# Expert mixture in a bidirectional encoder: V row weights built per four rows, and three more row buffers

## The reference

```
q = (xb @ wq)                      # 8 heads, 2 halves of 128
s = q . keys                       # 128 scores per half
top 16 of each half, top 16 of the 256 sums -> idx: 128 experts per token
gate = softmax(best)
act  = gelu(einsum('ted,td->te', u_tab[idx], xb)) * gate
out  = einsum('te,ted->td', act, v_tab[idx])
y    = rmsnorm(h + out)
```

## Time and profile before

| | us |
|---|---|
| median of 3 runs | 3148.33 |
| lowest, highest | 3132.29, 3150.12 |
| profiled execution, span from first to last instruction | 3149.3 |
| PE busy (matmul) | 2885.8 (92%) |
| PEld busy | 1456.1 (46%) |
| DVE busy | 1640.8 (52%) |
| ACT busy | 571.5 (18%) |
| POOL busy | 1538.7 (49%) |
| bytes moved | 1006.58 MB, mean 320 GB/s |

### The profile page before, as it was taken

The page is one execution under the profiler, slowest core; times in us unless marked ns, Lnnn a source line. Parts: engine busy times, 40 slices in busy tenths (PEclk is TensorE's granted clock), DMA queues, the critical chain, the costliest instruction groups (busy, mean ns, idle before and its releaser), DMA issues.

```text
span 3149.3 us, 30263 instructions
## 1 busy us (share of the span) xinstructions
PE 2885.8 (92%) x10618; PEld 1456.1 (46%) x10618; DVE 1640.8 (52%) x3896; ACT 571.5 (18%) x1212; POOL 1538.7 (49%) x1334
## 2 busy tenths in 40 slices
PE   6999989678999979956799999999999999999997
PEld 4656647433334445534344444444444444444442
DVE  5331125774887746887355654444655544444442
ACT  4111122110104556656000000000000000000000
POOL 3111213364565535655556565555555555555544
PEclk9999999899999999977899999999999999999999
DMA  4332264497999989999999999999999999999987
GB/s 150 110 104 74 87 213 143 140 372 259 334 392 355 367 339 382 364 343 404 400 367 376 384 385 366 379 381 378 385 388 394 382 368 376 384 369 390 373 335 293
DMA packets 341662, 1006.58 MB, mean 320 GB/s; under 512 B 32295, under 2 KB 110887, under 8 KB 338952
## 3 DMA queue, kind: packets, MB, share of 16 engines
q0 software_dynamic: 184320, 671.17, 56.0%
q1 hardware_dynamic: 155464, 308.32, 27.9%
q10 hardware_dynamic: 1728, 25.17, 1.9%
HBM read 958.13 MB, written 46.40 MB: 319 GB/s over the span
## 4 chain that ended last, share of the span: by engine, by line
PE 63%; DMA 9%; DVE 3%; issue 2%; POOL 1%; another core or an unknown queue 1%; ACT 1%; SPq 1%; POOLq 0%; DVEq 0%; ACTq 0%
PE job_ps L1627 20%; PE wide_ps L1611 19%; PE v_ps L1653 8%; PE job_ps L678 4%; PE wide_ps L678 4%; DMA v_rows<-in_peer_v,row_t 3%; PE gate_ps L678 2%; DMA u_row<-in_peer_u,row_u 2%; DMA arena<-in_peer_v 1%; DVE u_row L1870 1%; DMA hand<-tmp_gates 1%; PE job_ps L1599 1%; PE wide_ps L1599 1%; POOL v_rows L1535 1%
## 5 line engine op out<-in xcount | busy, mean ns | idle before, releaser
L1535 POOL DMA_INDIRECT v_rows<-in_peer_v,row_t x622 | 679.3, 1092 | 849.7 <-PE v_ps L1653 692.6
L1870 DVE CUSTOM_DVE_ANT_0 u_row<-u_row,x_tile 128x1024 f32<-128x1024 f32 x640 | 774.5, 1219 | 316.5 <-DMA u_row<-in_peer_u,row_u 287.2
L1520 POOL DMA_INDIRECT u_row<-in_peer_u,row_u x640 | 723.9, 1131 | 256.9 <-issue 191.8
L1627 PE MATMUL job_ps<-arena 128*128 128x512 f32 x1536 | 692.5, 599 | 8.2 <-issue 4.1
L1611 PE MATMUL wide_ps<-hand,arena 128*128 128x384 f32 x2048 | 687.5, 489 | 0.0
L1611 PEld LDWEIGHTS wide_ps<-hand,arena 128*128 128x128 f32 x2048 | 384.3, 190 | 317.7 <-issue 79.1
L1627 PEld LDWEIGHTS job_ps<-arena 128*128 128x128 f32 x1536 | 287.9, 191 | 376.2 <-issue 339.5
L1653 PE MATMUL v_ps<-v_rows,diag 128*32 128x512 f32 x2488 | 347.4, 613 | 44.2 <-DMA v_rows<-in_peer_v,row_t 40.8
L1912 DVE TENSOR_TENSOR arena<-arena,job_ps 128x512 f32<-128x512 f32 x192 | 131.2, 684 | 408.6 <-PE job_ps L1627 336.8
L948 POOL TENSOR_TENSOR exact<-arena,exact 128x1024 fp32r<-128x1024 f32 x48 | 116.7, 2436 | 437.7 <-ACT exact L690 437.7
L1760 ACT ACTIVATE hand<-wide_ps 128x384 f32<-128x384 f32 x128 | 62.7, 490 | 1413.9 <-PE wide_ps L1611 1176.0
(11 more groups left out here) (292 smaller groups left out, 2487.2 us busy)
## 6 DMA issues: line engine op xcount, KB each, us to landing
arena<-in_peer_ut SPq DMA_DIRECT2D x128, 512.0 KB
arena<-in_peer_v SPq DMA_DIRECT2D x128, 512.0 KB
hand<-tmp_gates SPq DMA_DIRECT2D x32, 768.0 KB
tmp_gates<-arena ACTq DMA_DIRECT2D x10, 2048.0 KB
arena<-in_w_in SPq DMA_DIRECT2D x32, 512.0 KB, 3.6
hand<-in_w_in SPq DMA_DIRECT2D x32, 512.0 KB
x_tile<-tmp_xn SPq DMA_DIRECT2D x80, 128.0 KB
u_row<-in_peer_u,row_u POOLq DMA_INDIRECT x640
```

What stands on the lines that cost most here:

```text
L1520: pool.indirect_dma_start(u_row[n % NU][:], None, dram["peer_u"], bass.IndirectOffsetOnAxis(row_u[g % 2][:, e:e + 1], 0)).then_inc(u_in[n ...
L1535: pool.indirect_dma_start(v_row[b], None, dram["peer_v"], bass.IndirectOffsetOnAxis(row_t[g % 3][:, t:t + 1], 0)).then_inc(v_in[b], 16)
L1627: last = pe.matmul(job_ps[q % 2][:], actd[g % 2][:, jj, d * P:(d + 1) * P], vw[j % NO][:, half * 512:(half + 1) * 512], start=jj == 0, sto ...
L1870: dve.tensor_tensor_reduce(out=u_row[n % NU][:], in0=u_row[n % NU][:], in1=xb[h_ % 2][:], scale=1.0, scalar=0.0, op0=ALU.mult, op1=ALU.add ...
```

## The change

`diag` goes, with ACT's zeroing of it. `turn_act` is followed by `keep_act(h)`, a copy of the turned activations (128x32) into a ring of eight, `act_t`. For each quad DVE then does `pick(n)`: it multiplies a slice of `unit_col`, a row of zeros with a one at place 31, by the four activation columns of the quad (128x4, broadcast over 32), which gives the four 128x32 weights, in one of `NP` = 4 small tiles `picked`. The quad waits for its pick (`picked_done`, once a quad, where `diag_done` was waited for once in eight). Pick n waits for `keep_act` of its 32 rows and for the quad four before it (`v_used`). In DVE's order it stands at beat 41 + 4n, ahead of the adds, dense steps and dot of that beat. The memory goes to the row buffers: `NU` 6 to 7, `NV` 7 to 9, and 16 instead of 13 for the last V rows.

```diff
-    NU, NV, NSC, NW, NO = 6, 7, 2, 3, 6
+    NU, NV, NSC, NW, NO = 7, 9, 2, 3, 6
+    NP, NH = 4, 8
...
-        diag = m.sb("diag", [P, Q, 32 * 32])
+        act_t = m.sb("act_t", [P, NH * QT])
+        unit_col = m.sb("unit_col", [P, 63])
+        picked = [m.sb(f"picked{b}", [P, Q, 32]) for b in range(NP)]
...
             def quad(n):
                 g, k = n // 32, n % 32
-                c = k % 8 * 4 + k // 8
-                if k % 8 == 0:
-                    pe.wait_ge(diag_done, n // 8 + 1)
+                pe.wait_ge(picked_done, n + 1)
...
-                        last = pe.matmul(v_ps[half][32 * q:32 * q + 32, :], diag[:, q, 32 * c:32 * c + 32],
+                        last = pe.matmul(v_ps[half][32 * q:32 * q + 32, :], picked[n % NP][:, q],
                                          v_row[v_home(r)][:, half * 512:(half + 1) * 512], start=k == 0, stop=k == 31)
...
-            act.activation(diag[:].rearrange("p q (a b) -> p (q a) b", b=P),
-                           R.iota[:].unsqueeze(1).broadcast_to([P, 32, P]), ACT.Copy, scale=0.0).then_inc(cleared, 1)
...
-            def set_diag(h):
+            def keep_act(h):
                 dve.wait_ge(act_turned, h + 1)
-                if h >= 4:
-                    dve.wait_ge(v_used, (h - 3) * QT)
+                if h >= NH:
+                    dve.wait_ge(picked_done, (h - NH + 1) * 8)
+                dve.tensor_copy(act_t[:, h % NH * QT:(h % NH + 1) * QT], act_ps).then_inc(act_t_done, 1)
+
+            def pick(n):
+                h, at = n // 8, n % 8
+                c = at * 4 + h % 4
+                dve.wait_ge(act_t_done, h + 1)
+                if n >= NP:
+                    dve.wait_ge(v_used, Q * (n - NP + 1))
                 else:
-                    dve.wait_ge(cleared, 1)
-                dve.tensor_copy(diag[:, :, 33 * (h % 4)::132], act_ps.rearrange("p (q c) -> p q c", q=Q)).then_inc(diag_done, 1)
+                    dve.wait_ge(unit_set, 2)
+                mine = act_t[:, h % NH * QT:(h % NH + 1) * QT].rearrange("p (q c) -> p q c", q=Q)[:, :, at:at + 1]
+                dve.tensor_tensor(picked[n % NP][:], unit_col[:, 31 - c:63 - c].unsqueeze(1).broadcast_to([P, Q, 32]),
+                                  mine.broadcast_to([P, Q, 32]), ALU.mult).then_inc(picked_done, 1)
...
+            dve.memset(unit_col[:], 0.0).then_inc(unit_set, 1)
+            dve.wait_ge(unit_set, 1)
+            dve.memset(unit_col[:, 31:32], 1.0).then_inc(unit_set, 1)
...
                     if n == GEL_AT[h_] + 5:
-                        set_diag(h_)
+                        keep_act(h_)
+                if n >= LAG - 1 and (n - LAG) % Q == Q - 1 and (n + 1 - LAG) // Q < ROWS // Q:
+                    pick((n + 1 - LAG) // Q)
```

More of the change, by code:

```diff
@@ L1380, in second_and_experts @@
         rows_u_done, gates_turned, gate_q_done = (m.sem(f"e_{n}") for n in ("rows_u_done", "gates_turned", "gate_q_done"))
-        exp_done, gel_done, act_done, act_turned, diag_done, v_used, lead_done, gate_done = (m.sem(f"e_{n}") for n in (
-            "exp_done", "gel_done", "act_done", "act_turned", "diag_done", "v_used", "lead_done", "gate_done"))
+        exp_done, gel_done, act_done, act_turned, act_t_done, picked_done, v_used, lead_done, gate_done = (m.sem(f"e_{n}") for n in (
+            "exp_done", "gel_done", "act_done", "act_turned", "act_t_done", "picked_done", "v_used", "lead_done", "gate_done"))
         sel_turned, sel_copied, a_done, sq_done, b_done, d_done, hot_used, evicted = (m.sem(f"e_{n}") for n in (
@@ L1386, in second_and_experts @@
             "u_used", "gel_read", "weighted", "job_done", "summed"))
-        added, ms, root, inv, normed, stored, cleared, pre_gone = (m.sem(f"e_{n}") for n in (
-            "added", "ms", "root", "inv", "normed", "stored", "cleared", "pre_gone"))
+        added, ms, root, inv, normed, stored, unit_set, pre_gone = (m.sem(f"e_{n}") for n in (
+            "added", "ms", "root", "inv", "normed", "stored", "unit_set", "pre_gone"))
         order, unit, held = [], 0, ()
@@ L1634, in turn_act @@
                 turn_free()
-                tr_reader[:] = [diag_done, h + 1]
+                tr_reader[:] = [act_t_done, h + 1]
                 for j in range(4):
```

## The result

The changed kernel takes 3111.98 us (median of 5, 3104.07 to 3123.68) against 3145.37 us of before (median of 5). The ratio is 0.9906, 95% interval 0.9878 to 0.9935: about 0.9% faster. 3106 was forecast, within 3065 to 3147. The profiled execution spans 3113.9 us where the one before spanned 3149.3, 35.4 us less.

What follows compares the result with a forecast made beforehand. PE's matmuls were taken to bound the dense stretch, 96.6% of 1600 to 3000 us. The terms -14 (dense stretch), -20 (600 to 1600 us) and -8 (tail) sum to -42 us: 3106 us against a median of 3148.3, range 3065 to 3147.

Steps and rivals of the forecast that it cites:

- the dense stretch: 1600 to 3000 us: one quad more of lead removes most of 16.3 us of landing waits, -14 us (ends 0 and -48).
- the early part: 600 to 1600 us: POOL, its U gathers and DVE get further ahead; -13 and -10 with +3 for picks, -20 us.
- the tail: From 3000 us: 16 homes instead of 13 let the last V gathers issue without a stop, -8 us (ends 0 and -12).
- What bounds the kernel: 1600 to 3000 us: unchanged matmul time fills 1352 of 1400 us, so at most 48 us can go.
- the -10 given to the engines' unused share: 600 to 1300 us: a fifth of the 48 us that the transfer engines leave unused is gained, -10 us.
- the 13 us of the way to 404 GB/s: 1300 to 1600 us: half of the 19 us up to the best slice's rate, plus the three-row reserve, -13 us.
- The step on POOL: Tail: the last 37 V gathers at 1.26 us each, 45 us to the start of the last instead of 53.6.
- Picks: Weights on DVE: 160 picks of 0.28 us, 45 us, just in time where DVE is late; charged 3 us (ends 0 and 15).
- U buffer: U buffers 6 to 7: nothing of its own; keeps U from becoming the next stop as POOL runs ahead.
- transfers are the bound: Rival, chance 0.28: 380 GB/s is all this mix gets, so V rows come no sooner; 3126 to 3143, say 3138 us.
- The late dense loads: Rival, chance 0.08: more rows in flight delay each dense V tile's landing by 3.4 us, 105 us over 31 groups; 3231 us.
- the early stage open up: Rival, chance 0.12: from 600 to 1600 us earlier dots end PE's waits for DVE and its clock recovers; 3068 us.

## Why the prediction was right, point by point

In the profiled executions the sum of -42 us became -35.4: the dense stretch gave more than its term, the early part and the tail less, so the errors partly cancel. The range to 3147 us reached past the kernel before (3145.37), so that the time lies in it says little; what carries the prediction is where the time came from.

**What bounds the kernel.** Right. In the dense stretch PE's own work was put at 1352 of 1400 us and the ceiling of any gain at 48 us. Taking transfers away from it brought nothing, and taking work from PE did. How much work PE could lose before the transfers take over was left open; of 83 us taken away 33 came out.

**The dense stretch, -14 us forecast, -17.3 measured.** The sum ran by the bounds 1600 and 3000 us, so it is compared at the quads nearest to them: the one that started at 1597.6 us starts 12.9 us earlier in the changed kernel, the one of 2996.4 us 30.2 earlier, and the end comes 35.4 earlier. That leaves 17.3 us for this stretch. The mechanism and nearly the size were right: the idle time that went is the 16.3 us that had been read before the V matmuls. (The 21.1 us between the first and the last product hold 3.1 more from after 3000 us.)

**600 to 1600 us, -20 forecast, -12.9 measured.** The mechanism was right, POOL further ahead by what the V buffers hold, and the 264.8 us at V gathers became 225.6 us in 38 places. At 1293.5 us the V quads were 9.6 us early, as much as the -10 given to the engines' unused share. What the 13 us of the way to 404 GB/s promised did not come: in 1300 to 1540 us the transfers carried 374, not more than before, and between 1293.5 and 1597.6 us the quads gained 3.3. Landings had ended 22.1 us of idle time from 1540 to 1600 and ended none there afterwards, but that alone moved little.

**The tail, -8 forecast, -5.2 measured from 3000 us on.** The step on POOL failed. From the first start of the last 37 V gathers to the last it is 53.1 us in the changed kernel (3035.8 to 3088.9) and 53.3 in the old, where 45 were forecast. Two things were missed. The sum took the 37 gathers as free of stops once the waits for quads were gone. Of the waits for PE in the old kernel three did go (3.06, 0.82 and 0.81 us). But the wait for one quad (the one that starts at 3071.6 us in the old kernel and at 3038.4 in the new) stands before row 603 in the old, just ahead of the last 37, and before row 605 in the new, inside them: 2.55 us. And stops whose cause the profile does not name stand in both kernels, 3.17 and 1.57 us before and 2.96 and 2.00 after; they did not go with more buffers, and what they are stays open. In the new kernel some gathers also took longer, 1.99 and 1.28 us the most, beside DVE's passes (the last section). At the very end the last V matmuls ran at the lower clock, 5.04 us for 12 where 1.92 us for 10 had ended the kernel before; that is 3.1 us.

**Picks.** Their duration (283 ns for 0.28 us) and their place were right; that they'd come just in time from 1300 to 1600 us was too: 17.3 us of PE's idle time are put down to them, all between 1300 and 1540. The prediction had named idle time of PE ended by picks there as a sign that the early part would come to nothing; the sign came and the early gain did not go. The 3 us charged for the picks are more than the earlier picks gave back, which is nothing that can be measured. The extra wait per quad can't be seen in the products' stretch (1567.8 with picks, 1568.6 without).

**U buffer, 0 forecast.** Right alone (0.9977 against 0.9981), and beside 9 V buffers (0.9906 against 0.9900 with 6). With 8 V buffers two more U buffers may be worth something: 0.9884 against 0.9924, intervals that just overlap.

**The rivals.** That transfers are the bound is refuted for the dense stretch. The late dense loads did not come: landings of dense V tiles ended 4.8 us of idle time before the jobs (5.6 in the earlier trace rows). Nor did the early stage open up: in 1300 to 1540 us PE was busy 159.4 us (166.1 before) and its clock stood at 0.83 (0.84 before), and with 6 and 10 buffers at 0.82.

**What the prediction did not see** is how the gain hangs on V = 8. A quad takes four rows. With 8 buffers all four rows of the next one can be fetched while PE still has to start this one; with 7 the fourth of them waits until this quad has used its first row, and in the dense stretch must then land, through full transfers, in what is left of the time between two quads. That time is 14.5 us in the median of the kernel before and 10.6 us in fifteen of 90 cases. One of these (PE's line of one quad, POOL's gather of the fourth row of the next, PE's line of the next; start, length):

```profile
2142.86 1.92 PE L1653 MATMUL v_ps<-v_rows,diag 128*32 128x512 f32 x16
2145.04 0.96 POOL L1535 DMA_INDIRECT v_rows<-in_peer_v,row_t  x1 [3.35 <-PE v_ps L1653]
2153.51 1.92 PE L1653 MATMUL v_ps<-v_rows,diag 128*32 128x512 f32 x16
```

That leaves 8.5 us, and the landings at the end of the two kernels took 8.46 and 9.45 us. The last column of the table shows the step: the fourth row starts 2.7 to 2.9 us sooner before its quad from 6 to 7 buffers, 6.9 from 7 to 8 (at 6 U buffers), 1.8 from 8 to 9 and 0.9 from 9 to 10; with 7 it starts less than 10 us before its quad in 18 of 90 cases, with 8 or more in none. The prediction had the rule for the fourth row but put it wrong for 9: it named the end of quad n-2, and that is where the row waits with 8; with 9 it waits for the third row of that quad, which is used in the same moment. So it didn't see that the ninth buffer adds nothing there. For V = 6 the same rule, asked forward, misled me: two rows wait instead of one, and I expected little since I took them to be 1.3 us apart. But a U gather stands between two V gathers, and the fourth row starts 9.4 us before its quad in the median, under 10 us in 47 of 87 cases. POOL stands with the U gathers behind it too: the dots wait 480.5 us for U rows instead of 271.4 with 6 and 7, and the transfers fall to 362 GB/s at a share of 0.97. Which part of the 3% each makes up was not tried.

## What to carry to other kernels

Count row buffers in units of what the consumer takes at once. With a consumer that takes four, the edge was at twice four: beside 6 U buffers the seventh V buffer was worth 3.3%, the eighth 0.6%, and beyond it next to nothing was left in the dense stretch. This is one kernel, and a consumer of another size was not tried; what to look at is the time from the issue of the last row to its use against the time that a landing takes. Before memory is freed for more buffers, move the split of those that are there: 5 and 8 instead of 6 and 7 gave three quarters of this gain. And a wait that a profile shows beside full transfers, like that for the picks, may be worth nothing: another can stand behind it.

## What the runs showed of the hardware

Gathers on POOL take longer when they begin while DVE runs an operation whose two inputs are in SBUF. In the kernel before, around 2112 us (start, length, engine, line):

```profile
2112.66 1.23 DVE L1870 CUSTOM_DVE_ANT_0 u_row<-u_row,x_tile 128x1024 f32<-128x1024 f32 x1 [1.23 <-DMA u_row<-in_peer_u,row_u]
2112.96 1.74 POOL L1520 DMA_INDIRECT u_row<-in_peer_u,row_u  x1 [0.30 <-issue]
...
2116.25 0.94 POOL L1520 DMA_INDIRECT u_row<-in_peer_u,row_u  x1 [0.30 <-issue]
2117.39 0.56 DVE L1900 TENSOR_TENSOR arena<-hand 128x384 f32<-128x384 f32 x1 [3.49 <-ACT hand L1760]
2117.50 1.25 POOL L1535 DMA_INDIRECT v_rows<-in_peer_v,row_t  x1 [0.31 <-issue]
```

Of the 720 gathers of 1600 to 3000 us, the 380 that begin with DVE idle take 0.940 us in the mean, the 206 that begin inside a dot 1.447, ending 0.80 us after the dot; the 46 that begin inside the job sums, which read one input from PSUM, 0.939. In the changed kernel the 12 that begin inside a pick take 1.024 us. The Trainium skill, "SBUF — State Buffer", section "SBUF: two separate sides", says that a DVE operation with two SBUF inputs and a GpSimd operation that reads SBUF take the same ports in turn, the second one blocked; the trace agrees. From 1600 to 3000 us POOL stands longer than that in its waits for PE, so it probably cost nothing there; in the tail, where POOL's gathers end the kernel, the longer ones add up to 1.7 us over 0.94 each in the changed kernel and 0.6 in the old. No run took this away.

The transfers reach 393 GB/s over 1300 us where PE lets them (share 1.03), on one core alone. That is above the limit of about 358 GB/s at which the HBM side binds by the Trainium skill, "DMA: Bandwidth & Descriptors", section "Where 436 GB/s comes from". The same page of the Trainium skill, section "Measured (HBM→SBUF, 128 partitions, SWDGE, issued from GpSimd)", says that each core gets this much when both cores of a pair stream, and lists higher rates for one alone. These runs have one core at work and agree with that; what two would get they don't show.
